# RWKV projections of a hybrid decoder trunk: fp32 matmuls against three fp32r passes with weight tiles split on the chip

## Chip, core and metric

One Trainium2 chip, one NeuronCore of it. The metric is the device time of one execution in microseconds (us). The profile shows one execution of the same program.

## What is computed

Two layers, each a mixer with three branches (RG-LRU, gated DeltaNet, RWKV-7) and a PEER retrieval layer, on 256 tokens of width 1024, all in float32. The change touches only the projections that are computed while the RWKV branch runs:

```python
z = xn @ w_in                         # xn: 256 x 1024
u_lru, g_lru, qkv, z_gdn, alpha, beta_pre, z_rw, z_merge = split(z)
zs = z_rw + mu * (shift(z_rw) - z_rw)
r, k, v, wl, al, gl = split(zs)
...
def step(state, inp):                 # RWKV, per head of 64 channels
    s_kk = einsum('bhvk,bhk->bhv', state, kk_t)
    state = state * w_t - s_kk * kka_t + v_t * k_t
    return state, einsum('bhvk,bhk->bhv', state, r_t)
```

## The kernel before

**Phases.** Each layer runs a norm, the RWKV phase (`rwkv_phase`), the DeltaNet phase, a merge, then the PEER phases. The change lies in the RWKV phase.

**Bodies.** The RWKV phase has a prologue and eight bodies, one for each block of 128 channels (two heads). Seven bodies are a hardware loop (`more=True`) and the eighth is written out after it (`more=False`). Every engine has its own part of a body: `pe_body`, `act_body`, `vec_body`, and a small `pool_body` that makes masks.

**Projections.** Eight weight tiles of 128 output channels by 1024 (512 KB) belong to a body: r, k and v for the block that comes next (`pe_piece`), and five side tiles f0 to f4 of this block (`pe_side`: inputs of the LRU branch and merge gates). A tile is eight fp32 matmuls, one for each k of 128 inputs, taken straight from the ring in SBUF, into which SP's DMAs load it. The trace shows two records for each fp32 matmul. A tile is cut into four parts of two k each, and the parts are spread by hand over the body, between the steps of the recurrence, whose matmuls wait for ScalarE and VectorE:

```python
for k in ks:
    mm = te.matmul(ps, ring[:, slot, k * P:(k + 1) * P], x[:, k, :], start=(k == 0), stop=(k == KT - 1))
```

**Order in a body on TensorE.** Head: the up-projections (L621 to L623), the norm of k (L625), transposes, then `side(0..7)` (all of f0 and f1) around L632, the transposes of L637, the 64-wide products of L648, and the first two parts of r. Inversion (`invert64_pe`): five levels of two steps each, `X` and then `Y`/`YT`; behind each step stands one part of r, k or v, ten in all. Recurrence: four chunks q = 0 to 3, with `side(8)` to `side(14)` between their steps. Tail: `side(15..18)`, a transpose (L704), `side(19)`.

**What orders the engines.** Each engine works its instructions in the order of the program, and counts steps in semaphores (`Steps`). In a body VectorE's chain and ScalarE's alternate: in the head ScalarE's sigmoid (L739), VectorE's scan (L819), ScalarE's exponentials and root (L746 to L750), VectorE's reciprocal and products (L834 to L842), TensorE's L637 and L648, VectorE's masks (L849 to L858), TensorE's L658. In an inversion step ScalarE copies X (L399), or VectorE adds Y and YT (L408, L414). In the recurrence, chunk q's `Rs` (L869) is VectorE's, and TensorE's next product (L685) waits for it:

```python
te.matmul(b5[rows(hf), 0:P], KR[:, b, 0, rows(hf)], St, ...).then_inc(E.sem, E.one(f"R{q}"))
side(2 * q + 7)
te.wait_ge(V.sem, V.at(f"R{q}", i))
```

**Evictions.** ScalarE moves the side tiles out of PSUM (`act_side`, L574 to L579), and scales r, k and v (`act_piece`, L597), to which VectorE adds the token shift (`vec_piece`, L602). SP loads a tile again when TensorE has used the one before it in that slot.

Of the kernel before, what the change touches and what calls it, by code (L numbers as in the profile page):

```python
# [21 lines left out]
P = 128  # L22
T = 256
# [76 lines left out]
def _program(nc, ctx, A, out, book):  # L100
# [36 lines left out]
    ARENA = 32768  # L137
    arena = sb("arena", [P, ARENA])
    banks = [ctx.enter_context(nc.psum_tensor(f"bank{i}", [P, 512], F32)) for i in range(8)]
# [89 lines left out]
    def project(te, ps, slot, x=None, ks=range(KT)):  # L229

        x = xn if x is None else x
        for k in ks:
            mm = te.matmul(ps, ring[:, slot, k * P:(k + 1) * P], x[:, k, :], start=(k == 0), stop=(k == KT - 1))  # L233
        return mm

# [219 lines left out]
    def rwkv_phase(l):  # L455
# [12 lines left out]
        VA, SA, EA = steps("rwA_vec", True), steps("rwA_act", True), steps("rwA_pe", True)  # L468
        V, S, E, G = steps("rwB_vec", True), steps("rwB_act", True), steps("rwB_pe", True), steps("rwB_pool", True)
        VF, SF, EF = steps("rwF_vec", True), steps("rwF_act", True), steps("rwF_pe", True)  # L470
# [23 lines left out]
        mu4, va4 = r_(4), r_(4)  # L494
        c = {n: k for k, n in enumerate(RWKV_COLS)}
# [11 lines left out]
        with nc.Block() as block:  # L507
            @block.sync
            def _(sp):
# [9 lines left out]
                with sp.Fori(1, NI) as i:  # L519
                    for s, what in enumerate("rkv"):  # L520
                        sp.wait_ge(EA.sem, EA.before(what, i))
                        rwkv_tile(sp, l, i, s)
                    sp.wait_ge(E.sem, E.before("gate", i))
                    sp.dma_start(small, A["rwkv_up"][l, i]).then_inc(loaded[3], 16)
                    for n in range(5):
                        sp.wait_ge(EF.sem, EF.before(f"f{n}", i))
                        rwkv_side_tile(sp, l, i, n)

                for s, what in enumerate("rkv"):
                    sp.wait_ge(EA.sem, EA.at(what, NI - 1))  # L530
                    gdn_tile_a(sp, l, 0, s)
                sp.wait_ge(EF.sem, EF.at("f0", NI - 1))
                gdn_tile_a(sp, l, 0, 3)
                for n in range(4):
                    sp.wait_ge(EF.sem, EF.at(f"f{n + 1}", NI - 1))
# [3 lines left out]
            def pe_piece(te, i, j, first=False):  # L539
                s, part = divmod(j, 4)  # L540
                if part == 0:
                    te.wait_ge(loaded[s], 16 * i + 16)

# [4 lines left out]
                mm = project(te, ps_in[s], s, ks=range(2 * part, 2 * part + 2))  # L548
                if part == 3:
                    mm.then_inc(EA.sem, EA.one("rkv"[s]))  # L550

            def pe_side(te, i, js, more):
                for j in js:
                    n, part = divmod(j, 4)
                    if part == 0:
                        te.wait_ge(loaded_f[n], 16 * i + 16)

# [8 lines left out]
                    mm = project(te, f_bank[n], F_SLOT + n, ks=range(2 * part, 2 * part + 2))  # L567
                    if part == 3:
                        mm.then_inc(EF.sem, EF.one(f"f{n}"))

            def act_side(a, i, n):
                a.wait_ge(EF.sem, EF.at(f"f{n}", i))
# [18 lines left out]
            def act_piece(a, i, s):  # L591
# [4 lines left out]
                a.wait_ge(EA.sem, EA.at("rkv"[s], i))  # L596
# [9 lines left out]
            def pe_body(te, i, more):  # L606
# [7 lines left out]
                if more:  # L614
                    EA.begin()
                EF.begin()
# [35 lines left out]
                fill(0, 1)  # L652
                te.wait_ge(S.sem, S.at("BK", i))
# [54 lines left out]
                EF.end()  # L708
                if more:
                    EA.end()  # L710

            @block.tensor
            def _(te):
# [3 lines left out]
                EA.prime(te)  # L717
                E.prime(te)
                EF.prime(te)
                EA.begin()  # L720
                for j in range(12):
                    pe_piece(te, 0, j, first=True)
                EA.end()
# [5 lines left out]
            def act_body(a, i, more):  # L729
                def fill(n):  # L730
                    if more and n in (2, 4):
                        act_piece(a, i + 1, n // 2 - 1)

# [16 lines left out]
                a.activation(rs, rs, ACT.Sqrt).then_inc(S.sem, S.one("rs"))  # L750
                a.wait_ge(E.sem, E.at("vT", i))
# [3 lines left out]
                act_side(a, i, 1)  # L755
                a.wait_ge(E.sem, E.at("bkT", i))
# [6 lines left out]
                for q in range(T // CH):  # L763
# [19 lines left out]
            def _(a):  # L783
                a.wait_ge(V0.sem, V0.at("made"))
# [10 lines left out]
                a.wait_ge(pload, 80)  # L795
                SA.begin()
                for s in range(3):
                    act_piece(a, 0, s)
                SA.end()
                with a.Fori(0, NI - 1) as i:  # L800
# [3 lines left out]
            def vec_body(v, i, more):  # L804
                def fill(n):
                    if more and n in (2, 4):
                        vec_piece(v, i + 1, n // 2 - 1)

# [1398 lines left out]
```

## Time and profile before

| | us |
|---|---|
| three runs | 3606.27, 3603.34, 3603.01 (median 3603.34) |
| the profiled execution, its own time | 3612.38 |
| its span | 3610.4 |
| TensorE matmul busy | 3344.8 (93%) |
| VectorE busy | 1942.2 (54%) |
| ScalarE busy | 1428.6 (40%) |
| fp32 projections (the helper's line L233) | 1034.2 busy, 4,160 records, in all phases |

Busy shares are means over all phases. What a change in one phase is worth must be read there: which engine's step is the last to be ready at each place. A row of the timeline merges neighbouring instructions of one line; its first number is the start, the second the stretch from the first start to the last end; in brackets stands how long the engine had been idle and who released it.

### The profile page before, as it was taken

The page shows a single profiled execution, that of the slowest core. Times are in us where ns is not written, and L with a number is a line of the kernel's source. Part 1 is how long each engine was busy: PE and PEld are TensorE (multiplying, and loading weights), DVE is VectorE, ACT ScalarE, POOL GpSimd, SP SyncE. Part 2 cuts the span into 40 slices and gives each one's busy share as a digit, 9 for nine tenths or more (in the row PEclk, how much of TensorE's full clock was granted, in tenths as well). Part 3 has the DMA queues.
Part 4 walks back from the last instruction along what each step waited for, and adds up shares of the span by engine and source line. Part 5 has one row for each costly group of instructions (what it writes and reads, how often), then busy time and mean ns, then how long its engine had stood idle before and what let it go on. Part 6 is the DMA issues. An engine that isn't in the chain of part 4 may idle for free. (4 is left out here: it accounts for less than half of the span.)

```text
span 3610.4 us, 70861 instructions
## 1 busy us (share of the span) xinstructions
PE 3344.8 (93%) x24076; PEld 2836.1 (79%) x24076; DVE 1942.2 (54%) x4381; ACT 1428.6 (40%) x3129; POOL 144.2 (4%) x169
## 2 busy tenths in 40 slices
PE   8999979988999999999889999799889999999997
PEld 6767657777988799999867676577679888999996
DVE  3444435652687655555534444456417876555554
ACT  2222223320258555555432222342202775555554
POOL 0000000010000000000000000001000000000000
PEclk9999969999999999999999999899999999999999
DMA  3221212323322555555322212122133125555553
GB/s 120 90 78 65 95 49 71 115 72 110 128 72 77 187 189 186 186 186 186 140 104 88 90 58 91 66 88 93 65 151 105 59 95 194 188 186 186 186 186 116
DMA packets 122222, 433.12 MB, mean 120 GB/s; under 512 B 15745, under 2 KB 18049, under 8 KB 121345
## 3 DMA queue, kind: packets, MB, share of 16 engines
q1 hardware_dynamic: 122112, 431.74, 33.9%
q8 instruction: 60, 0.98, 0.1%
q14 instruction: 50, 0.40, 0.0%
HBM read 430.64 MB, written 1.05 MB: 120 GB/s over the span
## 5 line engine op out<-in xcount | busy, mean ns | idle before, releaser
L233 PE MATMUL bank<-arena,ring 128*128 128x256 f32 x4160 | 1034.2, 395 | 44.7 <-PEq L185 12.8
L233 PEld LDWEIGHTS bank<-arena,ring 128*128 128x128 f32 x4160 | 771.7, 194 | 177.0 <-issue 60.7
L1993 DVE TENSOR_TENSOR u_parts<-u_raw,u_parts 128x512 fp32r<-128x512 f32 x384 | 265.8, 693 | 448.4 <-ACT u_parts L1938 448.4
L1938 ACT ACTIVATE u_parts<-u_raw 128x512 fp32r<-128x512 f32 x384 | 242.2, 631 | 519.9 <-PE bank L1877 519.9
L1875 PE MATMUL bank<-xhigh,u_parts 128*128 128x256 f32 x1536 | 433.9, 282 | 1.7 <-DVE u_parts L1993 1.7
L1877 PE MATMUL bank<-xhigh,u_parts 128*128 128x256 f32 x1536 | 434.7, 283 | 0.0
L1876 PE MATMUL bank<-xlow,u_parts 128*128 128x256 f32 x1536 | 434.6, 283 | 0.0
L1875 PE MATMUL bank<-v_parts,act_high 128*128 128x512 f32 x1024 | 405.7, 396 | 11.9 <-DVE v_parts L1998 11.8
L1876 PE MATMUL bank<-v_parts,act_high 128*128 128x512 f32 x1024 | 404.3, 395 | 0.0
L1877 PE MATMUL bank<-v_parts,act_low 128*128 128x512 f32 x1024 | 401.6, 392 | 0.0
L1998 DVE TENSOR_TENSOR v_parts<-v_raw,v_parts 128x512 fp32r<-128x512 f32 x512 | 329.6, 685 | 17.7 <-ACT v_parts L1945 14.9
L1875 PEld LDWEIGHTS bank<-xhigh,u_parts 128*128 128x128 f32 x1536 | 294.1, 191 | 9.9 <-DVE u_parts L1993 2.5
L1876 PEld LDWEIGHTS bank<-xlow,u_parts 128*128 128x128 f32 x1536 | 294.1, 191 | 7.4
L1945 ACT ACTIVATE v_parts<-v_raw 128x512 fp32r<-128x512 f32 x512 | 291.8, 617 | 14.2 <-DMA v_raw<-in_v 12.8
L1877 PEld LDWEIGHTS bank<-xhigh,u_parts 128*128 128x128 f32 x1536 | 294.1, 191 | 0.0
L377 PEld LDWEIGHTS bank<-arena 64*64 64x64 f32 x5504 | 183.7, 136 | 82.8 <-issue 82.8
L1875 PEld LDWEIGHTS bank<-v_parts,act_high 128*128 128x128 f32 x1024 | 195.2, 191 | 50.7 <-DVE v_parts L1998 14.4
L377 PE MATMUL bank<-arena 64*64 64x64 f32 x5504 | 214.4, 224 | 18.4 <-ACT arena L399 11.3
L1877 PEld LDWEIGHTS bank<-v_parts,act_low 128*128 128x128 f32 x1024 | 194.5, 190 | 42.6
L1876 PEld LDWEIGHTS bank<-v_parts,act_high 128*128 128x128 f32 x1024 | 195.5, 191 | 33.1
L1782 ACT ACTIVATE onehot_cols<-onehot_cols,slot_gate 128x128 f32<-128x128 f32 x512 | 162.5, 393 | 5.0 <-DVE onehot_cols L1735 3.3
L408 DVE TENSOR_TENSOR arena<-arena,bank 128x256 f32<-128x256 f32 x104 | 43.8, 421 | 217.6 <-PE bank L377 217.6
(333 smaller groups left out, 4201.0 us busy)
## 6 DMA issues: line engine op xcount, KB each, us to landing
v_raw<-in_v SPq DMA_DIRECT2D x256, 512.0 KB, 3.3
u_raw<-in_u SPq DMA_DIRECT2D x192, 512.0 KB, 4.6
ring<-in_w_side SPq DMA_DIRECT2D x80, 512.0 KB, 3.3
ring<-in_w_gdn SPq DMA_DIRECT2D x64, 512.0 KB, 3.3
ring<-in_w_rwkv SPq DMA_DIRECT2D x48, 512.0 KB, 6.0
ring<-in_w_gdn_side SPq DMA_DIRECT2D x32, 512.0 KB, 3.3
ring<-in_u SPq DMA_DIRECT2D x32, 512.0 KB, 3.7
u_ring<-in_u SPq DMA_DIRECT2D x32, 512.0 KB, 3.3
```

Source lines behind the costliest of these rows:

```text
L233: mm = te.matmul(ps, ring[:, slot, k * P:(k + 1) * P], x[:, k, :], start=(k == 0), stop=(k == KT - 1))
L377: mm = te.matmul(view(out)[rows, m], left[rows, m], right[rows, m], start=True, stop=True)
L408: v.tensor_tensor(T_, T_, view(bY), ALU.add).then_inc(V.sem, V.one(f"inv{lev}T"))
L1782: a_.activation(cols(r)[:, u], cols(r)[:, u], ACT.Copy, scale=slotg[:, bass.ds(32 * i + 4 * r + u, 1)]).then_inc(cols_act, 1)
L1875: te.matmul(ps, f32r(w_hi), f32r(x_hi), start=start, stop=False, **kw)
L1876: te.matmul(ps, f32r(w_hi), f32r(x_lo), start=False, stop=False, **kw)
L1877: return te.matmul(ps, f32r(w_lo), f32r(x_hi), start=False, stop=stop, **kw)
L1938: a_.activation(f32r(u_hi[:, half(n)]), u_raw[:, r % 2, half(n)], ACT.Copy).then_inc(u_high, 1)
L1945: a_.activation(f32r(v_hi[r % 2][:, half(n)]), v_raw[:, r % 2, half(n)], ACT.Copy).then_inc(v_high, 1)
L1993: v.tensor_tensor(f32r(u_lo[:, half(n)]), u_raw[:, r % 2, half(n)], u_hi[:, half(n)], ALU.subtract).then_inc(u_low, 1)
L1998: v.tensor_tensor(f32r(v_lo[r % 2][:, half(n)]), v_raw[:, r % 2, half(n)], v_hi[r % 2][:, half(n)], ALU.subtract)\
```

## The change

Projections of the RWKV phase (the two low-rank ones excepted) run as three fp32r matmuls per k: rounded weight by rounded x, rounded weight by the rest of x, rest of the weight by rounded x. Both parts of x are made once at the phase's start. The parts of a weight tile are made for each tile, in halves of 512 columns: ScalarE writes the rounded half (`round`), VectorE the difference (`rest`). Two slots of parts take turns; a slot's half is written again when TensorE has used it (`used`). TensorE waits for `low`, ScalarE for the load and for `used`, VectorE for `high`; SP's next load into a ring slot waits for `low` and no longer for TensorE.

```diff
+        PRIME = 4
+        def round(self, a, raw, n, parity, halves=(0, 1)):
+            for half in halves:
+                a.wait_ge(self.used, 2 * n + half + 1)
+                a.activation(f32r(w_parts[:, 0, parity, self.cols(half)]), raw[:, self.cols(half)], ACT.Copy).then_inc(self.high, 1)
+
+        def rest(self, v, raw, n, parity, halves=(0, 1)):
+            for half in halves:
+                v.wait_ge(self.high, 2 * n + half + 1)
+                v.tensor_tensor(f32r(w_parts[:, 1, parity, self.cols(half)]), raw[:, self.cols(half)],
+                                w_parts[:, 0, parity, self.cols(half)], ALU.subtract).then_inc(self.low, 1)
+
+        def project(self, te, ps, n, parity, part):
+            if part % 2 == 0:
+                te.wait_ge(self.low, 2 * n + part // 2 + 1)
+            for k in range(2 * part, 2 * part + 2):
+                w_hi, w_lo = (f32r(w_parts[:, x, parity, k * P:(k + 1) * P]) for x in range(2))
+                x_hi, x_lo = (f32r(x_parts[:, x, k]) for x in range(2))
+                te.matmul(ps, w_hi, x_hi, start=(k == 0), stop=False)
+                te.matmul(ps, w_hi, x_lo, start=False, stop=False)
+                mm = te.matmul(ps, w_lo, x_hi, start=False, stop=(k == KT - 1))
+            if part % 2:
+                mm.then_inc(self.used, 1)
...
+        number = {"r": 0, "k": 1, "v": 2, "f0": 6, "f1": 7, "f2": 11, "f3": 12, "f4": 13}
+        tile = lambda what, i: 8 * i + number[what]
+        parity = lambda what: number[what] % 2
```

Where the halves are made in the bodies, ScalarE first and then VectorE (`act_round` and `vec_rest` do both halves unless halves are named):

```diff
                 a.activation(rs, rs, ACT.Sqrt).then_inc(S.sem, S.one("rs"))
+                if more:
+                    act_round(a, i + 1, "r")
...
                 act_side(a, i, 1)
+                if more:
+                    act_round(a, i + 1, "k")
...
+                    if n == 1 and more:
+                        act_round(a, i + 1, "v")
+                    if n == 3:
...
+                        act_round(a, i, "f2")
+                    if n == 5:
+                        act_round(a, i, "f3")
...
+                    if q == 1:
+                        act_round(a, i, "f4")
...
+                if more:
+                    act_round(a, i + 1, "f0")
                 act_side(a, i, 3)
...
                 act_side(a, i, 4)
+                if more:
+                    act_round(a, i + 1, "f1")
```

```diff
                 v.scalar_tensor_tensor(rk, Z[:, 0], col(i, "r_k"), kp, ALU.mult, ALU.mult).then_inc(V.sem, V.one("rk"))
+                vec_rest(v, i, "f1")
...
                 v.tensor_tensor(bv, b7[:, 0:T], Z[:, 2], ALU.mult).then_inc(V.sem, V.one("bv"))
+                if more:
+                    vec_rest(v, i + 1, "r")
...
                 vec_taps(v, i)
+                if more:
+                    vec_rest(v, i + 1, "k")
...
+                    if n == 2 and more:
+                        vec_rest(v, i + 1, "v")
+                    if n == 4:
...
+                        vec_rest(v, i, "f2")
...
+                    if q == 0:
+                        vec_rest(v, i, "f3")
+                    if q == 2:
+                        vec_rest(v, i, "f4")
...
                 v.tensor_tensor(O4, O4, bc(va4), ALU.mult).then_inc(V.sem, V.one("on"))
+                if more:
+                    vec_rest(v, i + 1, "f0", (0,))
...
                 v.tensor_tensor(yc[:, i], y, gt, ALU.mult).then_inc(V.sem, V.one("y2"))
+                if more:
+                    vec_rest(v, i + 1, "f0", (1,))
```

In the prologue TensorE primes `used` behind the low-rank projections, waits for both halves of x, and projects r, k and v of block 0; ScalarE rounds x, r and k ahead of everything else, then v, and f0 and f1 behind the three `act_piece`; VectorE makes the rests in the same order.

How the order moves at three places. Names: `w_parts` are the split slots, `ring` the loaded tiles, `bank` PSUM, `arena` all other buffers; `rwB_...` are the body's step semaphores.

ScalarE, from chunk 3 to the end of the loop and the table load of the next sigmoid. Before:

```order
L768 ACTIVATE arena<-bank 64x128 [waits rwB_pe]
L572 REGISTER_ALU
L579 ISA [waits rwF_pe]
L579 ACTIVATE zg<-bank,arena 128x256
L774 REGISTER_ALU
L775 ACTIVATE arena<-arena 128x4 [waits rwB_vec]
L572 REGISTER_ALU
L579 ISA [waits rwF_pe]
L579 ACTIVATE zg<-bank,arena 128x256
L800 REGISTER_ALU
L800 COMPARE_AND_BRANCH
```

Now (L645 is the eviction that was L579):

```order
L645 ACTIVATE zg<-bank,arena 128x256
L851 REGISTER_ALU
L852 ACTIVATE arena<-arena 128x4 [waits rwB_vec]
L286 REGISTER_ALU
L645 ISA [waits rw_w_used]
L645 ACTIVATE zg<-bank,arena 128x256
L261 ISA [waits rwF_tile1]
L262 ACTIVATE w_parts<-ring 128x512 [waits rw_w_used]
L261 REGISTER_ALU
L262 ACTIVATE w_parts<-ring 128x512 [waits rw_w_used]
L885 REGISTER_ALU
L885 COMPARE_AND_BRANCH
```

Both halves of f1's rounding now stand between the last eviction and the next body's sigmoid.

VectorE, chunk 0 to chunk 1 of the recurrence. Before:

```order
L882 TENSOR_TENSOR arena<-arena,bank 64x128 [waits rwB_act]
L601 REGISTER_ALU
L602 ISA [waits rwA_act]
L602 SCALAR_TENSOR_TENSOR arena<-bank,arena 128x255
L868 REGISTER_ALU
L869 TENSOR_TENSOR arena<-bank,arena 64x128 [waits rwB_pe]
L871 TENSOR_SCALAR arena<-arena 128x128
```

Now:

```order
L978 TENSOR_TENSOR arena<-arena,bank 64x128 [waits rwB_act]
L667 REGISTER_ALU
L668 ISA [waits rwA_act]
L668 SCALAR_TENSOR_TENSOR arena<-bank,arena 128x255
L266 ISA
L267 TENSOR_TENSOR w_parts<-ring,w_parts 128x512 [waits rw_w_high]
L266 REGISTER_ALU
L267 TENSOR_TENSOR w_parts<-ring,w_parts 128x512 [waits rw_w_high]
L964 REGISTER_ALU
L965 TENSOR_TENSOR arena<-bank,arena 64x128 [waits rwB_pe]
L967 TENSOR_SCALAR arena<-arena 128x128
```

Both rests of f3 stand ahead of chunk 1's `Rs` (L869, now L965), for which TensorE waits; f4's rests stand so ahead of chunk 3's.

TensorE, the first `Y` step of the inversion and the part behind it. Before:

```order
L387 REGISTER_ALU
L377 MATMUL bank<-arena 64x64 [waits rwB_act]
L377 MATMUL bank<-arena 64x64 x15
L233 MATMUL bank<-arena,ring 128x256 x2
L382 REGISTER_ALU
```

Now:

```order
L444 REGISTER_ALU
L434 MATMUL bank<-arena 64x64 [waits rwB_act]
L434 MATMUL bank<-arena 64x64 x15
L279 MATMUL bank<-x_parts,w_parts 128x256
L280 MATMUL bank<-x_parts,w_parts 128x256
L281 MATMUL bank<-x_parts,w_parts 128x256
L279 MATMUL bank<-x_parts,w_parts 128x256
L280 MATMUL bank<-x_parts,w_parts 128x256
L281 MATMUL bank<-x_parts,w_parts 128x256
L439 REGISTER_ALU
```

A part of a tile was two instructions (four records) and is now six; its place is the same.

## Rows read from the trace of the kernel before

**Rows 1.** Windows: us, busy (records) PE, PEld, DVE, ACT, POOL, granted clock, DMA share, GB/s

```profile
41.60:430.80 389.20, 371.85 (x3543) 276.02 (x3542) 175.71 (x441) 103.23 (x224) 27.21 (x35) 1.00 0.21 74
...
462.00:485.90 23.90, 23.49 (x76) 14.84 (x76) 4.00 (x14) 1.17 (x4) 0.00 (x0) 0.50 0.07 23
```

**Rows 2.** Timeline, first and last projections of bodies, both layers

```profile
41.58 0.48 PE L621 MATMUL bank<-arena 64*128 64x256 f32 x1
...
430.84 0.45 PE L621 MATMUL bank<-arena 64*128 64x256 f32 x1
...
490.71 1.03 PE L233 MATMUL bank<-arena,ring 128*128 128x256 f32 x4
...
2231.15 0.45 PE L621 MATMUL bank<-arena 64*128 64x256 f32 x1
...
2281.05 1.03 PE L233 MATMUL bank<-arena,ring 128*128 128x256 f32 x4
```

**Rows 3.** Timeline, a Y step of the inversion, and the part behind it

```profile
284.71 1.13 PE L233 MATMUL bank<-arena,ring 128*128 128x256 f32 x4
...
285.77 1.15 PE L377 MATMUL bank<-arena 64*64 64x64 f32 x32
...
286.97 0.42 DVE L414 TENSOR_TENSOR arena<-arena,bank 128x256 f32<-128x256 f32 x1
...
287.91 0.68 PE L377 MATMUL bank<-arena 64*64 64x64 f32 x16
```

**Rows 4.** Timeline, dense streams: fp32 in the head, fp32r in the expert phase

```profile
266.77 2.76 PE L233 MATMUL bank<-arena,ring 128*128 128x256 f32 x12
...
270.08 4.48 PE L233 MATMUL bank<-arena,ring 128*128 128x256 f32 x20
...
1501.45 0.28 PE L1875 MATMUL bank<-xhigh,u_parts 128*128 128x256 f32 x1
...
1504.33 0.40 PE L1875 MATMUL bank<-v_parts,act_high 128*128 128x512 f32 x1
```

**Rows 5.** Timeline, splitting of weight tiles in the expert phase, two halves each

```profile
1499.75 1.14 ACT L1945 ACTIVATE v_parts<-v_raw 128x512 fp32r<-128x512 f32 x2
...
1500.51 1.29 DVE L1998 TENSOR_TENSOR v_parts<-v_raw,v_parts 128x512 fp32r<-128x512 f32 x2
1501.72 0.42 DVE L2022 TENSOR_TENSOR slots<-slots,arena 128x256 f32<-128x256 f32 x1
```

**Rows 6.** Timeline, head of body 4

```profile
264.17 0.47 ACT L579 ACTIVATE zg<-bank,arena 128x256 f32 x1 [2.18 <-PE bank L233]
...
264.77 1.28 ACT L739 ACT_TABLE_LOAD   x1
...
271.28 1.75 DVE L834 RECIPROCAL arena<-arena 128x256 f32<-128x256 f32 x1 [1.30 <-ACT arena L750]
...
276.46 0.76 DVE L849 TENSOR_TENSOR arena<-bank,made_of_shapes 128x256 f32<-128x256 f32 x2 [1.04 <-PE bank L648]
...
278.68 0.55 PEld L658 LDWEIGHTS bank<-made_of_shapes,arena 64*64 64x64 f32 x16 [0.33 <-issue]
```

**Rows 7.** Timeline, recurrence of body 4: chunks 0 to 1 and 2 to 3

```profile
301.79 0.48 DVE L602 SCALAR_TENSOR_TENSOR arena<-bank,arena 128x255 f32<-128x255 f32 x1
...
302.31 0.29 DVE L869 TENSOR_TENSOR arena<-bank,arena 64x128 f32<-64x128 f32 x1
...
303.15 0.44 PE L685 MATMUL bank<-arena 64*64 64x64 f32 x4
...
310.98 0.27 DVE L882 TENSOR_TENSOR arena<-arena,bank 64x128 f32<-64x128 f32 x1
...
311.59 0.29 DVE L869 TENSOR_TENSOR arena<-bank,arena 64x128 f32<-64x128 f32 x1 [0.34 <-PE bank L679]
...
312.55 0.44 PE L685 MATMUL bank<-arena 64*64 64x64 f32 x4
```

**Rows 8.** Timeline, last body of layer 1, ahead of its inversion

```profile
445.31 0.68 PE L658 MATMUL bank<-made_of_shapes,arena 64*64 64x64 f32 x16 [1.81 <-issue]
```

More of the change, by code:

```diff
@@ L234, in project, with __init__, cols, free @@
         return mm
+    class Split:
+        PRIME = 4
+        def __init__(self, name):
+            self.high, self.low, self.used = (lsem(f"{name}_{x}") for x in ("w_high", "w_low", "w_used"))
+        def cols(self, half):
+            return slice(half * KT * P // 2, (half + 1) * KT * P // 2)
+        def round(self, a, raw, n, parity, halves=(0, 1)):
[7 more added lines that the diff above has]
+                                w_parts[:, 0, parity, self.cols(half)], ALU.subtract).then_inc(self.low, 1)
+        def free(self, sp, n):
+            sp.wait_ge(self.low, 2 * n + 2)
+        def project(self, te, ps, n, parity, part):
[9 more added lines that the diff above has]
+                mm.then_inc(self.used, 1)
+        def done(self, engine, n):
+            engine.wait_ge(self.used, self.PRIME + 2 * n + 2)
+        def skip(self, engine, sem, n, tiles, prime=0):
+            engine.wait_ge(sem, prime + 2 * n)
+            engine.sem_inc(sem, 2 * tiles)
     def softplus_exp(a, S, x, e, tag):
@@ L520, in _ @@
                     for s, what in enumerate("rkv"):
-                        sp.wait_ge(EA.sem, EA.before(what, i))
+                        W.free(sp, tile(what, i - 1))
                         rwkv_tile(sp, l, i, s)
@@ L547, in pe_piece @@
                         te.wait_ge(*((SF.sem, SF.at("f0", i - 1)) if s == 0 else (VF.sem, VF.at("tap3", i - 1))))
-                mm = project(te, ps_in[s], s, ks=range(2 * part, 2 * part + 2))
-                if part == 3:
-                    mm.then_inc(EA.sem, EA.one("rkv"[s]))
+                W.project(te, ps_in[s], tile("rkv"[s], i), parity("rkv"[s]), part)
             def pe_side(te, i, js, more):
@@ L566, in pe_side, with act_round, vec_rest @@
                             te.wait_ge(*((VF.sem, VF.at("tap3", i)) if n == 2 else (SF.sem, SF.at("f0", i))))
-                    mm = project(te, f_bank[n], F_SLOT + n, ks=range(2 * part, 2 * part + 2))
-                    if part == 3:
-                        mm.then_inc(EF.sem, EF.one(f"f{n}"))
+                    W.project(te, f_bank[n], tile(f"f{n}", i), parity(f"f{n}"), part)
+            def act_round(a, i, *whats):
+                for what in whats:
+                    s = "rkv".find(what)
+                    a.wait_ge(loaded[s] if s >= 0 else loaded_f[int(what[1])], 16 * i + 16)
+                    W.round(a, ring[:, s if s >= 0 else F_SLOT + int(what[1])], tile(what, i), parity(what))
+            def vec_rest(v, i, what, halves=(0, 1)):
+                s = "rkv".find(what)
+                W.rest(v, ring[:, s if s >= 0 else F_SLOT + int(what[1])], tile(what, i), parity(what), halves)
             def act_side(a, i, n):
-                a.wait_ge(EF.sem, EF.at(f"f{n}", i))
+                W.done(a, tile(f"f{n}", i))
                 if n == 0:
@@ L652, in pe_body @@
                 fill(0, 1)
+                if not more:
+                    W.skip(te, W.used, tile("r", NI), 3, W.PRIME)
                 te.wait_ge(S.sem, S.at("BK", i))
@@ L783, in _ @@
             def _(a):
+                for k in range(0, KT, KT // 2):
+                    a.activation(f32r(x_parts[:, 0, k:k + KT // 2]), xn[:, k:k + KT // 2], ACT.Copy).then_inc(x_high, 1)
+                act_round(a, 0, "r", "k")
                 a.wait_ge(V0.sem, V0.at("made"))
@@ L807, in fill @@
                         vec_piece(v, i + 1, n // 2 - 1)
+                    if n == 2 and more:
+                        vec_rest(v, i + 1, "v")
+                    if n == 4:
+                        if not more:
+                            W.skip(v, W.low, tile("r", NI), 3)
+                        vec_rest(v, i, "f2")
                 tt = lambda o, a0, a1, op, label=None: v.tensor_tensor(o, a0, a1, op).then_inc(V.sem, V.one(label))
```

54 lines of the change are left out of this document (34 added, 20 removed).

## The prediction

> **What bounds the kernel now.** I read the windows of the RWKV phase first, then the timeline of one body. Over the seven looped bodies of a layer TensorE is busy 371.85 of 389.2 us, VectorE 175.7, ScalarE 103.2 [rows 1]. From the first matmul of body 0 to that of body 7 it is 430.84 - 41.58 = 389.3 us [rows 2], 55.6 us a body. So TensorE is the bound by its share; but it works a chain whose steps wait for the other two, and its projections are filling between the steps. A shorter filling shortens a body only where the other engine's step is ready before the filling ends. In the inversion it is: behind the step of 285.77, VectorE's last addition ends at 286.97 + 0.42 = 287.39, and TensorE goes on at 287.91, 0.5 us later, when its part of a tile is through [rows 3]. In the head and in the tail it is not: there VectorE and ScalarE are late and TensorE idles, and work that is added to them there is paid in full.
>
> **The cheaper projection.** In a dense stream of fp32, eight records more take 4.48 - 2.76 = 1.72 us, so 0.215 us a record and 0.43 us a k. The fp32r stream of the expert phase puts 24 matmuls of the same shape between 1501.45 and 1504.33: 0.120 us each, 0.36 us for the three of a k [rows 4]. A part (two k) that stands between steps takes 285.77 - 284.71 = 1.06 us [rows 3], of which 4 x 0.215 = 0.86 us is streaming and 0.20 us the exposed weight load and the end. I keep the 0.20 us, since it belongs to every change between two kinds of matmul there: the new part is 6 x 0.12 + 0.20 = 0.92 us, 0.145 us less. The bounds are 0 (the six short matmuls don't reach the dense rate in so short a group) and 0.21 us (the fixed part shrinks too, with the shorter last matmul).
>
> **The price of splitting.** Per tile ScalarE does two halves of 512 columns, 1.14 us from first start to last end; VectorE two, 1.29 us, and its next instruction starts 1.21 us after the first [rows 5]. Eight tiles a body make 9.1 us of ScalarE and 9.7 us of VectorE, which both have idle time enough [rows 1]. What counts is where they stand.
>
> **Body, step by step** (times of body 4, 263.96 to 319.55).
>
> *Head.* f1's rounding now stands between ScalarE's last eviction and the sigmoid. The eviction starts at 264.17; with `side(19)` 0.15 us shorter, at 264.02. The next ScalarE instruction can start 0.37 us on, the two halves take 1.14 us, so the table load for the sigmoid starts at 265.55 in place of 264.77 [rows 6]: **+0.78 us**, and everything to L637 hangs on the sigmoid. f0's second rest stands ahead of VectorE's first two steps (+0.6 us), but its scan waits for the sigmoid anyway, so this is covered. f1's rests (1.21 us) lie in the 1.30 us that VectorE waits for ScalarE's root before its reciprocal [rows 6]: nothing. r's rests stand ahead of the masks, which wait 1.04 us for TensorE's 64-wide products [rows 6]; 1.21 us minus that and the margin between steps is about 0.1 us, of which I add 0.02. The chain reaches L658 **0.80 us** later than 278.68. The first two parts of r (0.3 us less) lie in that wait and give nothing. Queued behind r's and k's rounding on ScalarE are the copies of L753 and L757, both early. Without the cover in the head, f1's and r's rests would cost 1.2 us each.
>
> *Inversion.* Ten parts, **-1.45 us**. ScalarE rounds v, f2 and f3 behind the copies of levels 1, 3 and 5; the second half waits until the part just before the next step has been used, and is through about 0.15 us before the next copy is due. VectorE has 2.5 us between a YT and the next Y, and k, v and f2 need 1.21 us each. Both costs are nothing as long as a level takes 3.8 us.
>
> *Recurrence.* `side(8)`, `(10)`, `(11)`, `(12)`, `(14)`: 5 x 0.145 = **-0.73 us**. In chunks 1 and 3 it turns: f3's rests go ahead of `Rs` of chunk 1. VectorE's shift starts at 301.79, the rests at 302.2, so `Rs` starts at 303.41 and not at 302.31, and TensorE's next product at 303.75 in place of 303.15 [rows 7]: **+0.60 us**. f4's rests start behind L882 at 311.17, `Rs` at 312.38 and not 311.59, TensorE at 312.72 in place of 312.55 [rows 7]: **+0.17 us**. There the shorter filling gives nothing.
>
> *Tail.* VectorE's norm is the bound; the parts beside it lie under it. f0's first rest (0.6 us) stands in VectorE's wait for the transpose, about as long. Nothing.
>
> A body: 0.80 - 1.45 - 0.73 + 0.60 + 0.17 = **-0.61 us**, 14 looped bodies -8.5 us. The last body of a layer has no parts in its inversion, so only its recurrence gains: +0.89 (no earlier wait hides a part of the rounding) - 0.73 + 0.4 - 0.15 = +0.4 us, twice: +0.8 us. The prologue projects three tiles 2 us faster, but v waits behind x's, r's and k's splitting and ScalarE's activations, and f0's and f1's roundings (2.2 us) stand ahead of body 0's sigmoid: I come to +0.1 us a layer, taking it that TensorE's priming of `used` is issued before its low-rank matmuls are done; were it not, r's rounding starts 4 us later, +2.8 us. I take +0.2 us for both layers. The DMAs: SP now reloads a slot when it is split, which is before TensorE used to be done; every tile is loaded at least 8 us before its rounding. Nothing.
>
> Sum: -8.5 + 0.8 + 0.2 = **-7.5 us**. The profiled execution took 3612.38 us, so 3604.9 beside it. It lies 9.0 us above the median, and the rows say why: layer 1's last body runs from 430.84 to about 491, 60 us, layer 2's from 2231.15 to about 2281, 50 us [rows 2], since in the first the granted clock is 0.50 from 462 to 486 [rows 1], the lower level of 1.2 GHz. The runs of the median are taken to be without it. So 3603.34 - 7.5 = 3595.8 us. Of this kernel a measurement can tell about 0.2% (7.2 us) from no change; the forecast lies just at that.
>
> **Rivals.**
>
> *The small group does not shrink (slower).* Place: the 15 parts of a looped body that stand between steps. Price: if six fp32r matmuls behind a change of kind take 1.06 us as four fp32 records do, the body is 0.80 + 0.77 = +1.57 us, 14 of them +22.0, last bodies +2.6, prologue +0.2: 3628 us. It decides below 0.11 us gained per part (220 parts, 24.8 us). For it: no row shows a lone group of six fp32r. Against: the dense rows.
>
> *The clock falls in the heads (slower).* TensorE idles some 1.5 us more in a head. In the last body it idles 1.81 us ahead of L658 [rows 8], and in layer 1 the clock is at 1.2 GHz shortly after. If it fell for some 3.4 us in each head and cost half of that, 1.7 x 14 = +24: 3620 us; in half of them 3608. Against: all looped bodies are at 1.00 [rows 1] with gaps of their own.
>
> *Handovers cost more.* Each half adds two waits; 0.5 us a body more on the path eats all: 3603 us.
>
> *More is gained.* A part gains the full 0.21 us: 220 x 0.065 = 14 us more, 3582 us. To that the skill's 109 ns would come as well; the rows give it little.
>
> **Chances.** Forecast 0.55 (own range 3588 to 3602), more gained 0.08, handovers 0.18, group 0.12, clock 0.07. Of the forecast some two thirds fall beyond 0.2%: faster 0.37 + 0.08 = 0.45. Same: 0.18 + 0.17 = 0.35. Slower: 0.20, the group, the clock and the worst of the handovers. The range, 3581 to 3612 us, leaves out the group case, half of the clock case and a little below.
>
> **What would show it.** Bodies of 55.0 us in place of 55.6; parts between steps of 0.92 us; the sigmoid's table load some 1.5 us behind the eviction's start; TensorE waiting for VectorE at L658 (now L723) and, in chunks 1 and 3, at L685; rests of f1 inside the wait for the root. Wrong if the level of the inversion stays at 3.8 us (no gain per part; it should be 3.5), if ScalarE's copies of X are late behind a half that waits for `used`, or if the granted clock in looped bodies is below 1.00.

## The result: slower, 3670.8 us

| | before | change |
|---|---|---|
| median of 4 runs, us | 3604.02 (3603.01 to 3606.27) | 3670.82 (3665.66 to 3677.89) |
| ratio | | 1.0186, 95% interval 1.0165 to 1.0206 |
| profiled execution, us (span) | 3612.38 (3610.4) | 3667.03 (3665.2) |
| mean granted clock | 0.967 | 0.942 |

3595.8 us was forecast, with a range up to 3612. The change costs 67 us where it was to give 7.5. The two profiled executions differ by 55 us, since the one of before took 8 us more than its median and the one of the change 4 us less; the account below is of these 55 us. The next lines are the windows of the changed kernel: the seven looped bodies of layer 1, which answer to [rows 1]; then of body 4 its head, inversion, recurrence up to U3 (the products of chunk 3 that wait for `Rs`: L685, now L750), and the 6.8 us behind it; last a stretch of body 5.

```profile
39.90:456.50 416.60, 375.66 (x3990) 318.33 (x3991) 243.48 (x554) 165.22 (x338) 27.34 (x35) 0.89 0.21 73
279.45:295.03 15.58, 11.99 (x109) 10.19 (x109) 13.65 (x28) 11.70 (x21) 1.41 (x2) 1.00 0.22 76
295.03:313.70 18.67, 18.67 (x333) 16.58 (x333) 10.26 (x22) 6.38 (x14) 2.50 (x4) 1.00 0.04 10
313.70:328.12 14.42, 11.93 (x87) 9.20 (x86) 6.70 (x19) 3.32 (x8) 0.00 (x0) 1.00 0.17 60
328.12:334.94 6.82, 6.82 (x34) 6.03 (x32) 3.19 (x10) 2.10 (x5) 0.00 (x0) 0.50 0.87 283
...
375.90:396.40 20.50, 19.99 (x85) 15.95 (x86) 6.43 (x20) 4.32 (x10) 0.00 (x0) 0.50 0.34 116
```

The same three windows of body 4 in the kernel before (head, inversion, recurrence):

```profile
263.96:278.69 14.73, 13.41 (x90) 10.17 (x89) 10.90 (x23) 8.59 (x15) 1.40 (x2) 1.00 0.64 222
278.69:298.88 20.19, 20.19 (x314) 15.59 (x313) 6.44 (x16) 3.58 (x9) 2.49 (x4) 1.00 0.00 0
298.88:312.77 13.89, 12.75 (x75) 8.62 (x74) 4.31 (x15) 1.63 (x5) 0.00 (x0) 1.00 0.10 38
```

Two things are to be seen. Up to the recurrence the body does what was forecast: head 15.58 for 14.73 us, inversion 18.67 for 20.19. And the granted clock of the looped bodies, 1.00 before, is 0.89: from within the recurrence on there are stretches at 0.50, which is 1.2 GHz. The timeline gives the starts of bodies 1 to 5:

```profile
97.92 0.48 PE L684 MATMUL bank<-arena 64*128 64x256 f32 x1
...
159.94 0.48 PE L684 MATMUL bank<-arena 64*128 64x256 f32 x1
...
217.45 0.48 PE L684 MATMUL bank<-arena 64*128 64x256 f32 x1
...
279.45 0.48 PE L684 MATMUL bank<-arena 64*128 64x256 f32 x1
...
336.95 0.48 PE L684 MATMUL bank<-arena 64*128 64x256 f32 x1
```

Bodies take 62.0 and 57.5 us in turn (seven long and seven short ones over both layers; layer 2 begins with two long ones), where all took 55.6 [rows 2]. In a long one the clock is low for 20.5 us from chunk 1 on, in a short one for 6.8 us from chunk 3 on; these two are called the long and the short fall. Over both layers the 14 looped bodies take 838.1 us, 59.9 each; before it was 778.5. The two last bodies together take 105.6 for 109.3 us (in both kernels one of the two has some 25 us at the low clock). 59.6 - 3.7 = 55.9 us, and the spans differ by 54.8: the loss lies in the looped bodies of RWKV.

The timeline of body 4, chunk 1 and chunk 3, shows where the clock falls; it answers to [rows 7] (L965 was L869, L750 was L685, L978 was L882):

```profile
316.25 0.27 DVE L978 TENSOR_TENSOR arena<-arena,bank 64x128 f32<-64x128 f32 x1
...
316.45 0.48 DVE L668 SCALAR_TENSOR_TENSOR arena<-bank,arena 128x255 f32<-128x255 f32 x1
...
316.85 1.28 DVE L267 TENSOR_TENSOR w_parts<-ring,w_parts 128x512 fp32r<-128x512 f32 x2
...
318.16 0.29 DVE L965 TENSOR_TENSOR arena<-bank,arena 64x128 f32<-64x128 f32 x1
...
318.60 0.41 PE L750 MATMUL bank<-arena 64*64 64x64 f32 x4 [0.89 <-DVE arena L965]
...
326.14 1.28 DVE L267 TENSOR_TENSOR w_parts<-ring,w_parts 128x512 fp32r<-128x512 f32 x2
...
327.45 0.29 DVE L965 TENSOR_TENSOR arena<-bank,arena 64x128 f32<-64x128 f32 x1
...
327.89 0.47 PE L750 MATMUL bank<-arena 64*64 64x64 f32 x4 [0.47 <-DVE arena L965]
...
328.90 0.58 PE L279 MATMUL bank<-x_parts,w_parts 128*128 128x256 f32 x1
...
329.29 0.41 PE L280 MATMUL bank<-x_parts,w_parts 128*128 128x256 f32 x1
...
329.50 0.41 PE L281 MATMUL bank<-x_parts,w_parts 128*128 128x256 f32 x1
```

The rests of f3 and f4 stand ahead of `Rs`, so TensorE waits 0.89 us in chunk 1 and 0.47 us in chunk 3, and from one of the two on the matmuls stand 0.21 us apart, where it was 0.12. The same wait in body 5, in which the long fall begins, at 375.90:

```profile
376.10 0.66 PE L750 MATMUL bank<-arena 64*64 64x64 f32 x4 [0.89 <-DVE arena L965]
```

### The profile page after: what moved, and what is told of

The parts are those of the page before. It is cut to its first block and busy times, and to the rows that moved or that the text cites. A ratio compares the mean times of both kernels' runs of the same rounds, so it can differ in the third digit from the quotient of the medians.

```text
span 3665.2 us, 74133 instructions
## 1 busy us (share of the span) xinstructions
PE 3349.0 (91%) x25100; PEld 2928.4 (80%) x25100; DVE 2100.3 (57%) x4641; ACT 1573.5 (43%) x3389; POOL 144.5 (4%) x169
## 5 line engine op out<-in xcount | busy, mean ns | idle before, releaser
L244 PE MATMUL bank<-arena,ring 128*128 128x256 f32 x2112 | 502.2, 393 | 44.1 <-PEq L196 12.8
L244 PEld LDWEIGHTS bank<-arena,ring 128*128 128x128 f32 x2112 | 404.8, 196 | 107.2 <-issue 40.3
L279 PE MATMUL bank<-x_parts,w_parts 128*128 128x256 f32 x1024 | 353.0, 345 | 1.1 <-DVE arena L668 1.1
L280 PE MATMUL bank<-x_parts,w_parts 128*128 128x256 f32 x1024 | 313.0, 306 | 0.0
L281 PE MATMUL bank<-x_parts,w_parts 128*128 128x256 f32 x1024 | 311.7, 304 | 0.0
L279 PEld LDWEIGHTS bank<-x_parts,w_parts 128*128 128x128 f32 x1024 | 218.3, 213 | 40.6 <-issue 23.9
L262 ACT ACTIVATE w_parts<-ring 128x512 fp32r<-128x512 f32 x256 | 153.9, 624 | 198.4 <-PE bank L281 190.7
L1986 PEld LDWEIGHTS bank<-v_parts,act_high 128*128 128x128 f32 x1024 | 195.4, 191 | 51.0 <-DVE v_parts L2109 14.1
```

Source lines behind the costliest of these rows:

```text
L279: te.matmul(ps, w_hi, x_hi, start=(k == 0), stop=False)
L280: te.matmul(ps, w_hi, x_lo, start=False, stop=False)
L281: mm = te.matmul(ps, w_lo, x_hi, start=False, stop=(k == KT - 1))
L1986: te.matmul(ps, f32r(w_hi), f32r(x_hi), start=start, stop=False, **kw)
```

## The experiments

In the recurrence seven parts of a tile are now shorter by a seventh, and there are two new waits. Theories, as the expectations name them: **A**, TensorE's added waits for `Rs`, behind the rests of f3 and f4, let the clock fall; **B**, the shorter parts alone do, since they leave TensorE too little work; **C**, it has nothing to do with the recurrence (the later head, or ScalarE's and VectorE's new work). Each kernel is compared with the kernel before on the same chip.

### The waits taken out: e_moved

```diff
                         if q < 3:
                             v.tensor_scalar(SP, St, end, None, ALU.mult).then_inc(V.sem, V.one())
+                        if q == 1:
+                            vec_rest(v, i, "f3")
+                        if q == 3:
+                            vec_rest(v, i, "f4")
...
-                    if q == 0:
-                        vec_rest(v, i, "f3")
-                    if q == 2:
-                        vec_rest(v, i, "f4")
```

> The change with VectorE's rests of f3 and f4 moved out of the way of Rs: f3's behind Rs and the scaling of the state in chunk 1, f4's behind Rs in chunk 3, where VectorE waits 2.4 to 3 us for TensorE anyway. Theory A (the clock falls because TensorE waits 0.8 and 0.4 us more for Rs in chunks 1 and 3): the granted clock is 1.00 in all looped bodies, a body takes about 54.4 us (55.6 + 0.85 in the head - 1.5 in the inversion - 0.6 in the recurrence), 3604 - 17 = about 3587 us. Theory B (the shorter parts alone make the recurrence too thin for the clock): the falls stay, perhaps later in the body, some 4 us a body, 3640 to 3660 us. Theory C (the clock has nothing to do with the recurrence; other work is slower): falls as in the change, 3665 us.

Measured: 3585.86 us (3579.73 to 3592.64), ratio 0.9933 (0.9914 to 0.9952) to 3609.08. Windows of its looped bodies of layer 1, and of body 4's recurrence:

```profile
39.95:417.51 377.56, 339.89 (x3990) 288.22 (x3991) 244.18 (x554) 165.89 (x339) 27.33 (x35) 1.00 0.24 79
290.14:303.11 12.97, 11.83 (x86) 9.20 (x86) 6.20 (x19) 3.32 (x8) 0.00 (x0) 1.00 0.20 66
```

The same arithmetic with two pairs of subtractions at another place is 2.5% faster than the change (ratios 0.9933 and 1.0186 to before) and beats the kernel before. A holds against B and C: short parts and the new work are all still there. A body takes 53.85 us, the clock stays at 1.00, but for 3.4 us in the head of layer 2's first body. The recurrence is 12.97 for 14.4 us, so at full clock the two waits cost 1.4 us.

### Work added: e_fill and e_fill1

```diff
                         side(2 * q + 7)
+                        for _ in range({1: 4, 3: 2}.get(q, 0)):
+                            te.matmul(b4[:, 0:T], f32r(x_parts[:, 0, 0, 0:P]), f32r(x_parts[:, 0, 1]), start=True, stop=True)
                         te.wait_ge(V.sem, V.at(f"R{q}", i))
```

> The change with six more fp32r matmuls per body, four in chunk 1 and two in chunk 3, which write into a bank that nobody reads then; they stand where TensorE waits for Rs. No wait is taken away. Theory A in its wider form (idle time of TensorE at these two places makes the clock fall): the clock is 1.00 in the looped bodies, although there is more work; a body takes 55.3 to 55.5 us, 3600 us. Theory B: the six matmuls are worth 0.7 us of streaming against some 1.6 us that the eleven parts of the recurrence have lost, so the falls become fewer but stay: 3630 us or more. Theory C: no change, 3670 us.

e_fill1 has the four of chunk 1 alone:

> The change with four more fp32r matmuls, into the idle bank 4, in chunk 1's wait for Rs only (each of the seven looped bodies of both layers); chunk 3's wait stays empty. If each fall of the clock is set off by the gap in front of which it stands, the long falls (20.5 us, after chunk 1's wait) are gone and the short ones (6.8 us, after chunk 3's wait) stay: the bodies with a short fall stay near 57.5 us and the others become such ones too or stand at 55.3 us, so about 3604 + 14 x 2.2 = 3635 us if all have a short fall and 3617 us if every other has. If the stretch is judged as a whole, four matmuls lift it over the threshold and no looped body falls: 55.1 to 55.4 us a body, 3600 us. If the added work has nothing to do with it, 3670 us.

Measured: e_fill 3602.1 us (3598.17 to 3607.2), ratio 0.9981 (0.9971 to 0.999) to 3609.08; e_fill1 3611.42 us (3606.52 to 3619.95), ratio 1.0006 (0.9997 to 1.0016) to 3609.05. Windows of the looped bodies of layer 1, e_fill, and of its recurrence in body 4:

```profile
40.00:425.00 385.00, 343.59 (x4020) 291.73 (x4021) 241.32 (x548) 165.40 (x336) 27.30 (x35) 1.00 0.24 76
295.80:310.19 14.39, 12.63 (x92) 9.90 (x92) 6.70 (x19) 3.31 (x8) 0.00 (x0) 1.00 0.20 64
```

Six matmuls a body whose product nobody reads, set into waits whose ends stay where they were, make the change 2% faster, some 69 us. The recurrence takes the same 14.39 us with 12.63 us of TensorE in it for 11.93, a looped body 55.28 us, and none falls. That is the change at full clock: 55.28 for 55.60 us. With chunk 1 filled alone the long falls are gone, as expected; four of 14 bodies keep a short one (6.8 us low, 57.5 us), the others stand at 55.3 to 55.8 (the two first bodies have 3.4 us at the low clock in their heads). I had expected seven or more, or none.

### One wait at a time: e_wait1 and e_wait3

Each is e_moved with one of the two moves left out: f3's rest ahead of `Rs` in e_wait1, f4's in e_wait3.

> The change with the rest of f4 moved behind Rs (chunk 3) and the rest of f3 left ahead of it (chunk 1), so chunk 1's wait of 0.89 us alone is there. At full clock a body of about 54.8 us. If the wait in chunk 1 is enough for the long fall, low clock of 20.5 us in some looped bodies right behind it and 3600 to 3650 us; if it takes both waits, none and 3599 us.

> The other half: the rest of f3 moved behind Rs, that of f4 left ahead of it, so chunk 3's wait of 0.47 us alone is there. At full clock a body of about 54.3 us. If this wait is enough for the short fall, low clock of 6.8 us in some looped bodies from +48 us and 3600 to 3625 us; if it takes both waits, none and 3593 us.

Measured, in a single execution each: 3649.12 and 3600.7 us, beside 3609.13. Windows of the looped bodies of layer 1, e_wait1:

```profile
41.10:452.70 411.60, 372.86 (x3990) 315.44 (x3990) 244.00 (x554) 165.53 (x337) 27.31 (x35) 0.90 0.22 74
```

and e_wait3:

```profile
41.00:424.10 383.10, 344.09 (x3990) 292.00 (x3990) 243.27 (x554) 165.62 (x337) 27.30 (x35) 0.99 0.24 79
```

Chunk 1's wait is enough: eight of 14 bodies fall, for 17 or 20.5 us (the first of layer 1 has 3.4 us in its head besides), and take 60.7 to 62.5 us; the others take 54.75 (one 55.3). Chunk 3's makes two of 14 fall for 6.8 us (56.58 us); the others take 54.35 (the two first ones 54.8). At full clock the first wait costs 54.75 - 53.85 = 0.90 us, the second 0.50. How many bodies fall is counted in one execution each, here and below; in e_passwait, below, four executions of one kernel lie 30 us apart, with mean granted clocks of 0.941 to 0.955, so such a count is not a fixed one.

### The two halves of the change apart: e_passes and e_split

e_passes leaves the splitting out: `w_parts` is made once a layer, from r and k of block 0, and TensorE runs the three passes of every later tile on it, so its values are not the right ones.

```diff
         def project(self, te, ps, n, parity, part):
-            if part % 2 == 0:
-                te.wait_ge(self.low, 2 * n + part // 2 + 1)
...
             def vec_rest(v, i, what, halves=(0, 1)):
+                if not (isinstance(i, int) and i == 0 and what in "rk"):
+                    return
```

> The three fp32r passes alone: the weight parts are made once per layer, for r and k of block 0, and all later tiles are multiplied with these; so the splitting of all other tiles, and with it the right values, is left out, and TensorE waits for the loads as in the kernel before. Theory A: no waits for Rs, clock 1.00, a body about 55.6 - 1.5 - 0.9 = 53.2 us, 3604 - 34 = 3570 us. Theory B: the clock falls in the recurrence without any wait for VectorE; body 56 to 58 us, 3610 to 3640 us.

e_split does all the splitting, and multiplies in fp32 from the ring, as before:

```diff
-            for k in range(2 * part, 2 * part + 2):
...
-                te.matmul(ps, w_hi, x_hi, start=(k == 0), stop=False)
-                te.matmul(ps, w_hi, x_lo, start=False, stop=False)
-                mm = te.matmul(ps, w_lo, x_hi, start=False, stop=(k == KT - 1))
+            mm = project(te, ps, slot, ks=range(2 * part, 2 * part + 2))
```

> The splitting alone: ScalarE and VectorE make the parts of every tile at the same places and with the same waits, but TensorE multiplies in fp32 from the loaded tiles, once low is there; the ring is free again when TensorE is done. Theory A: the waits for Rs are there (0.6 and 0.2 us beyond the fp32 parts), so the clock falls as in the change, 3660 us or more. Theory B: TensorE's parts are as long as before, so the clock stays at 1.00, and the body takes 55.6 + 0.85 + 0.8 = 57.2 us, 3604 + 23 = 3627 us.

Measured: e_passes 3569.06 us (3561.18 to 3576.99), ratio 0.9884 (0.9867 to 0.99); e_split 3641.33 us (3638.39 to 3646.36), ratio 1.0093 (1.0076 to 1.0109), both to 3609.08. The recurrence of body 4 in e_passes:

```profile
285.39:298.35 12.96, 11.82 (x86) 9.19 (x86) 4.31 (x15) 1.65 (x5) 0.00 (x0) 1.00 0.12 40
```

and in e_split:

```profile
308.94:323.95 15.01, 12.84 (x74) 8.62 (x74) 6.70 (x19) 3.31 (x8) 0.00 (x0) 1.00 0.10 35
```

No looped body falls in either. So neither half does it alone, and A as I had put it, that the added waits suffice, doesn't hold in e_split. But its waits are also shorter than the change's, since the longer parts fill more of them. Its two products of body 4 that wait for `Rs`:

```profile
314.01 0.41 PE L745 MATMUL bank<-arena 64*64 64x64 f32 x4 [0.72 <-DVE arena L960]
...
323.76 0.41 PE L745 MATMUL bank<-arena 64*64 64x64 f32 x4 [0.32 <-DVE arena L960]
```

TensorE idles 0.72 and 0.32 us there, where it was 0.89 and 0.47. It takes the subtractions ahead of `Rs` and the short parts together; whether the short parts do more than to lengthen the two waits isn't shown, since no run has fp32 parts with the waits of the change. e_split's body takes 57.71 us for 55.60, all at full clock: head +1.0, recurrence +1.1, inversion 20.18 us for 20.19. Theory B forecast 57.2 us and 3627 us: the clock stayed as it said, but a body is 0.5 us and the run 14 us longer. The passes alone are worth 55.6 - 53.0 = 2.6 us a body.

### Short parts and the wait, without the splitting: e_passwait

```diff
+                    if q in (0, 2):
+                        for half in range(2):
+                            v.tensor_tensor(f32r(spare[:, W.cols(half)]), w_parts[:, 0, 1, W.cols(half)], w_parts[:, 0, 0, W.cols(half)], ALU.subtract).then_inc(V.sem, V.one())
```

> The three passes alone again (parts made once per layer, splitting left out, so the output is not the reference's), and in chunks 1 and 3 of every recurrence two subtractions of VectorE's 128x512 form into a spare buffer, at the place where the change has the rests of f3 and f4: nothing of the splitting but the wait for Rs that it makes. Theory (thin parts together with that wait let the clock fall, and nothing else is needed): looped bodies of 54.4 us at full clock plus falls as in the change (6.8 us and 20.5 us of low clock in turn), 56 to 61 us each, 3569 + 14 x 4 to 14 x 6 = 3625 to 3655 us. Rival (something else of the splitting is needed too, such as the later head with ScalarE's roundings in it): no low clock in looped bodies, 54.4 us each, 3590 us.

Measured: 3649.98 us (3628.75 to 3658.89), ratio 1.0108 (1.0064 to 1.0152) to 3609.13. Its looped bodies of layer 1, and body 4's recurrence:

```profile
39.30:446.40 407.10, 371.97 (x3990) 314.57 (x3990) 192.82 (x469) 103.24 (x223) 27.28 (x35) 0.90 0.22 71
309.59:328.24 18.65, 17.11 (x86) 13.23 (x86) 6.73 (x19) 1.66 (x5) 0.00 (x0) 0.65 0.09 28
```

Eight of 14 bodies fall, for 17.1 or 20.5 us, and take 59.9 to 61.3 us; the others take 54.45 to 54.56, with both waits in them. Its heads are those of before (14.76 us for 14.73; ScalarE rounds nothing in them), so the later head isn't needed for it. Short parts and VectorE's four subtractions ahead of `Rs` are all that it takes: 81 us over e_passes.

### A better version: e_best, and the last bodies: e_bestlast, e_beforelast

e_best is e_moved with f0 and f1 left unsplit; TensorE multiplies them in fp32 from the ring.

```diff
                 act_side(a, i, 4)
-                if more:
-                    act_round(a, i + 1, "f1")
...
-                    W.project(te, f_bank[n], tile(f"f{n}", i), parity(f"f{n}"), part)
+                    if n < 2:
+                        if part == 0:
+                            te.wait_ge(loaded_f[n], 16 * i + 16)
+                        mm = project(te, f_bank[n], F_SLOT + n, ks=range(2 * part, 2 * part + 2))
```

> The rests of f3 and f4 behind Rs, and f0 and f1 not split: TensorE multiplies them in fp32 from the ring, as the kernel before does, so ScalarE rounds nothing between the last eviction of a body and the sigmoid of the next (f2, f3, f4, r, k, v stay split, six tiles a body). By the theory that the rounding of f1 delays the head: T0 at +14.7 instead of +15.6 us, inversion and recurrence as with the rests moved (18.67 and 12.96 us), 53.0 us a looped body, no low clock there: 3586 - 14 x 0.85 - 2 = 3572 us. If the head is held by something else (the loads of f0 and f1, or the head's own vector work with the rests of r and k in it) it stays at +15.6 and the time at 3586. If the fp32 parts in the head cost there what they cost in the inversion, 8 x 0.14 us a body more: 3588 us.

Measured: 3573.37 us (3568.86 to 3576.53), ratio 0.9894 (0.9878 to 0.9911) to 3609.05. Windows of layer 1's looped bodies, and of layer 2's last body:

```profile
40.70:412.30 371.60, 348.11 (x3878) 288.61 (x3878) 227.83 (x525) 147.81 (x308) 27.31 (x35) 1.00 0.24 80
...
2185.32:2240.67 55.35, 47.98 (x475) 39.00 (x475) 26.92 (x65) 16.89 (x35) 3.88 (x5) 0.78 0.18 61
```

The product that was L658 and L723 starts 14.81 us into the body for e_moved's 15.60: the splitting of f0 and f1 is what the head pays, and eight fp32 parts in the head cost nothing. That it is f1's rounding ahead of the sigmoid fits the timeline of the head further below, but no run shows it alone: f0's rounding and both rests went out with it. A looped body takes 53.08 us. The last body of layer 2 still falls (0.78); layer 1's, without a fall, takes 46.81.

e_bestlast puts three unread fp32r matmuls behind each part's place in the inversion of the last bodies, e_beforelast one fp32 matmul there in the kernel before:

```diff
                     if more:
                         pe_piece(te, i + 1, 2 * lev + y)
+                    elif lev:
+                        for _ in range(3):
+                            te.matmul(banks[0][:, 0:T], f32r(x_parts[:, 0, 0, 0:P]), f32r(x_parts[:, 0, 1]), start=True, stop=True)
```

> The run before this one with three more fp32r matmuls of 256 columns, into the free bank 0, behind each of the ten parts of the inversion in the last body of each layer, where there is no next body whose projections would fill TensorE. Theory: what lets the clock fall in that body is the inversion without filler, so with filler the last bodies take 48 to 49 us in both layers with at most 3.4 us at the low clock; against e_best 8 to 10 us less for each layer in which e_best's last body falls (24 to 27 us at the low clock), 3556 to 3564 us, and the spread between runs shrinks. Rival: the recurrence behind the inversion is what falls, as in the change; then the last bodies keep their low stretches and the time is e_best's or up to 3 us above it (the added matmuls).

> The kernel before with one more fp32 matmul of 256 columns behind each of the ten parts of the inversion in the last body of each layer only. Before, one of the two last bodies took 59.65 us with 27.3 us at the low clock and the other 49.63. Theory: filler keeps the clock up, both stand near 49.5 us, 3604 - 5 to 10 = 3594 to 3599 us with less spread. Rival (one matmul of 0.48 us is too little, or the inversion is not what lets it fall): 3604 to 3610 us, and a last body with 24 to 27 us at the low clock remains.

Measured: e_bestlast 3568.26 us (3566.17 to 3569.96), ratio 0.9882 (0.9866 to 0.9899); e_beforelast 3613.01 us (3609.48 to 3617.39), ratio 1.0009 (0.9999 to 1.0019), both to 3609.05. The last body of layer 2 in e_bestlast:

```profile
2182.24:2231.93 49.69, 45.08 (x504) 36.64 (x504) 26.89 (x65) 16.90 (x35) 3.88 (x5) 0.97 0.19 65
```

The last bodies come near what was expected (48 to 49 us, and 49.5): 48.46 and 49.69 us for e_best's 46.81 and 55.35, and in e_beforelast 49.88 and 51.37 us for 59.65 and 49.63. No long low stretch is left in these four. But that the filler did it isn't shown: of the 22 last bodies of the other eleven kernels (before and the change among them), 15 had none either. The times do not follow: neither lies where its theory put it. e_bestlast's median is 5 us below e_best's, where 8 to 10 (3556 to 3564 us) were expected; e_beforelast was to take 3594 to 3599 us and is no faster than before, though its last bodies are 8 us shorter than the profiled ones of before. The stretches between and behind the RWKV phases, which no edit touches, are 1356 and 1337 us in it and were 1351 and 1332; over all profiles here they lie between 1349 and 1356, and 1331 and 1342. The clock varies there too (92 to 116 us at the low level between the phases, 91 to 111 behind), so a few us in the sum of a run say less than the bodies do.

## Why the prediction was wrong

- *Price of a part: right.* 0.92 us was said. The inversion of the changed kernel [rows 3]:

```profile
301.65 1.15 PE L434 MATMUL bank<-arena 64*64 64x64 f32 x32
...
302.73 0.39 PE L279 MATMUL bank<-x_parts,w_parts 128*128 128x256 f32 x1
302.95 0.28 PE L280 MATMUL bank<-x_parts,w_parts 128*128 128x256 f32 x1
303.07 0.28 PE L281 MATMUL bank<-x_parts,w_parts 128*128 128x256 f32 x1
...
303.64 0.68 PE L434 MATMUL bank<-arena 64*64 64x64 f32 x16
```

303.64 - 302.73 = 0.91 us, and the matmuls, each with a weight load beside it, follow each other by 0.12 us. The Trainium skill's 262 cycles, 0.109 us ("TensorE: Matmul & The Clock Gate", section "Back-to-back issue gap"), stand there for a matmul without weight loads; this stream has them, and the sum 14 us lower that the prediction worked out from that figure doesn't apply to it. The inversion gained 1.52 us for 1.45 forecast, a level takes 3.51 us for 3.81. "The small group does not shrink" is out.

- *Head: right.* The timeline of the head of body 4, which answers to [rows 6]:

```profile
279.88 1.14 ACT L262 ACTIVATE w_parts<-ring 128x512 fp32r<-128x512 f32 x2
281.03 1.28 ACT L808 ACT_TABLE_LOAD   x1
...
295.03 0.68 PE L723 MATMUL bank<-made_of_shapes,arena 64*64 64x64 f32 x16 [0.31 <-DVE arena L952]
```

The table load starts 1.53 us behind the eviction of 279.50, where 1.5 was said. L723 is 0.85 us later for 0.80, and e_best gives 0.79 us of it back.

- *Recurrence at full clock: mechanism right, size short.* To U3 it is 14.39 us (e_fill; 14.42 with the fall's start in it) for 13.89, +0.50; the terms up to there (four parts, both waits) made +0.19. The waits cost 0.90 and 0.50 us by the single experiments, where 0.60 and 0.17 stood. Part of that gap is my base: I measured the waits from the times of before, while e_moved, from which the experiments count, has also the gain of `side(9)` and `side(13)` (recurrence -0.92 us). From that base the forecast's waits are 0.60 + 0.145 = 0.75 and 0.17 + 0.145 = 0.32 us, so 1.40 - 1.07 = 0.33 us of the two together is what was missed. With all of it a looped body at full clock is 55.28 us for 55.0 forecast, 4.5 us less than before over 14 bodies; e_fill is 7 us below the kernel before.

- *The clock: the step that failed.* I had the fall as a rival, with 0.07, but put it into the heads, where TensorE idles longest, and took for its price 1.7 us a body, and dismissed it with "all looped bodies are at 1.00 [rows 1] with gaps of their own". The heads stay at 1.00 with 11.99 us of TensorE in 15.58 (only that of layer 2's first body has 3.4 us at the low clock). It is the recurrence that falls, the stretch from which the sum removed work and to which it added waits in the same paragraph. There TensorE's share went from 12.75 of 13.89 us to 11.93 of 14.42, and the sum had taken both changes only as time. The price was too small too: a long fall (20.5 us low) makes a body 62.02 - 55.28 = 6.7 us longer, a short one (6.8 us) 57.53 - 55.28 = 2.25 us, over all bodies 59.9 - 55.28 = 4.6 us, 14 x 4.6 = 64 us. With the -4.5 us at full clock and -3.7 of the last bodies it is 56 us, the difference of the spans. Of the low time a third is lost. One reason is shown: at the low clock matmuls fill waits that stand idle at full clock (in a long fall the 0.47 us of idle time ahead of chunk 3's product is gone); how much that makes in all isn't. The half that the Trainium skill counts ("TensorE: Matmul & The Clock Gate", section "HAM oscillation — how this bites in real kernels") would by my estimate be 10 us for a long one, where 6.7 were measured.

- *Handovers.* No cost of their own was seen beyond the places named: ScalarE's roundings in the inversion delay nothing: it takes 18.67 us in the change and 18.66 in e_passes, which has none of them.

**What stays open.** Why the bodies fall in turn, or eight of 14 in one kernel and two in another, isn't settled; the traces show only that a fall begins near one of the two waits: from 0.2 us before to 2.6 us behind the start of chunk 1's product, or 0.1 to 0.6 us behind that of chunk 3's. In bodies that don't fall the same waits stand at the same places. Nor is it settled why e_split, 12.84 us of TensorE in 15.01, never falls and e_wait1, 11.84 in 13.86, does in half of its bodies, so I give no rule by shares.

## What to carry to other kernels

When a change both shortens TensorE's filling and adds a wait in the same stretch, ask of that stretch whether the clock will hold, and not of the one with the longest gap: here the clock took 64 us, where the passes were worth 36 (14 x 2.6) and the two waits cost 20 (14 x 1.4). Side work of another engine goes behind the result that TensorE waits for, even where the delay looks like half a microsecond: moving two pairs of subtractions a body turned +67 us into -23, and leaving two of eight tiles unsplit, where splitting lay on the path, into -36. And when a granted clock below 1.00 shows in a stretch that is not bound by TensorE, try unread matmuls in its wait first: it is the cheapest test of whether the clock, and not the work, is what costs.

## What I had not expected of the hardware

- The clock falls to 1.2 GHz behind a stretch whose longest idle time of TensorE is 0.89 us, while the heads of the same bodies, with 3.6 us of idle time and 1.32 us of it in one piece, and the kernel before's recurrence stay at 2.4 GHz. With six matmuls more, 12.63 for 11.93 us of TensorE in the same 14.4, it did not fall.
- Either half alone, the short parts (e_passes) or the splitting with fp32 parts and its waits of 0.72 and 0.32 us (e_split), leaves the clock of the looped bodies at 1.00; one wait with the short parts brings it down in some of them.
- In six of the eleven kernels whose last bodies are not edited, the last body of one layer (in e_moved of both) has 24 to 27 us at the low clock and is some 8 us longer for it, now in layer 1 and now in layer 2, with the same instructions.
